# Where VectorE splits the next group's operands inside an up projection group: after two of its eight result additions instead of after four

## What is computed

```python
s = jnp.einsum("thpd,hpnd->thpn", q, keys)          # scores; top 16 of 256 pairs per head give idx and gate
pre = jnp.einsum("td,thkd->thk", xt, down[idx])
act = (jax.nn.gelu(pre.astype(jnp.float32), approximate=False) * gate).astype(xt.dtype)
return jnp.einsum("thk,thkd->td", act, up[idx])     # added to x
```

## Time and profile before

| what | value |
|---|---|
| median of 3 runs | 2968.42 us (2968.40 to 2971.78) |
| the profiled execution | 2967.73 us, of which the span is 2965.8 us |
| PE busy | 2742.1 us, 92% of the span |
| DVE busy | 1888.9 us, 64% |
| ACT busy | 1127.9 us, 38% |
| POOL busy | 1075.9 us, 36% |
| pure groups, layer 0 | 1226.44 to 1477.91 us |
| pure groups, layer 1 | 2693.76 to 2944.84 us |

### The profile page before, as it was taken

The page is one execution under the profiler, slowest core; times in us unless marked ns, Lnnn a source line. Parts: engine busy times, 40 slices in busy tenths (PEclk is TensorE's granted clock), DMA queues, the critical chain, the costliest instruction groups (busy, mean ns, idle before and its releaser), DMA issues.

```text
span 2965.8 us, 55557 instructions
## 1 busy us (share of the span) xinstructions
PE 2742.1 (92%) x20766; PEld 2529.3 (85%) x20766; DVE 1888.9 (64%) x3331; ACT 1127.9 (38%) x1682; POOL 1075.9 (36%) x444
## 2 busy tenths in 40 slices
PE   7899999989987999999988999999999889999997
PEld 5687777889987999999866877778999779999997
DVE  1663562299798554689817526533995975457887
ACT  1312320344487444333303124104445864443332
POOL 0000110478843656433300001004887245663332
PEclk9999999999999999999999999999999999999998
DMA  5222223255544566455452322233555446664543
GB/s 191 101 80 82 103 75 140 88 174 175 170 146 171 199 207 205 155 194 184 143 184 72 104 72 90 88 128 129 170 170 169 152 174 206 198 199 165 195 172 107
DMA packets 145453, 439.50 MB, mean 148 GB/s; under 512 B 62066, under 2 KB 63602, under 8 KB 126772
## 3 DMA queue, kind: packets, MB, share of 16 engines
q1 hardware_dynamic: 132548, 400.84, 39.7%
q10 hardware_dynamic: 12784, 37.00, 3.3%
HBM read 407.10 MB, written 30.15 MB: 147 GB/s over the span
## 4 chain that ended last, share of the span: by engine, by line
PE 61%; DVE 15%; issue 12%; POOL 8%; ACT 2%; DVEq 1%; DMA 0%; POOLq 0%; ACTq 0%; SPq 0%
PE banks L462 60%; POOL DHL L1903 7%; DVE arena L1356 3%; DVE OHE L1356 2%; DVE OHG L1356 2%; DVE ACTS L1356 1%; DVE AHL L1356 1%; ACT arena L983 1%; DVE UHL L1356 1%; POOL arena L1891 1%; DVE hT L1364 1%; DVE arena L1685 0%; DVE arena L1457 0%; DVEq L1356 0%; ACT L983 0%
## 5 line engine op out<-in xcount | busy, mean ns | idle before, releaser
L462 PE MATMUL banks<-HHL,DHL 128*128 128x264 f32 x6816 | 859.4, 287 | 23.6 <-POOL DHL L1903 12.1
L462 PEld LDWEIGHTS banks<-HHL,DHL 128*128 128x128 f32 x6816 | 844.2, 190 | 32.3 <-POOL DHL L1903 16.5
L462 PE MATMUL banks<-AHL,UHL 128*128 128x264 f32 x6144 | 773.3, 286 | 31.6 <-DVE AHL L1356 29.1
L462 PEld LDWEIGHTS banks<-AHL,UHL 128*128 128x128 f32 x6144 | 758.6, 189 | 41.9 <-issue 41.8
L1903 POOL TENSOR_TENSOR DHL<-ring,DHL 128x1024 fp32r<-128x1024 f32 x256 | 657.3, 2572 | 277.8 <-ACT DHL L983 276.0
L1356 DVE TENSOR_TENSOR xT<-xT,banks 128x264 f32<-128x264 f32 x1040 | 402.7, 423 | 388.8 <-PE banks L462 387.9
L462 PE MATMUL banks<-hT,ring 128*128 128x272 f32 (+1 forms) x2048 | 501.8, 403 | 9.7 <-issue 7.9
L1909 POOL TENSOR_TENSOR UHL<-ring,UHL 128x1024 fp32r<-128x1024 f32 x128 | 308.7, 2412 | 538.2 <-ACT UHL L983 538.2
L462 PEld LDWEIGHTS banks<-hT,ring 128*128 128x128 f32 x2048 | 394.4, 196 | 101.7 <-issue 23.1
L983 ACT ACTIVATE UHL<-ring 128x2048 fp32r<-128x2048 f32 x128 | 245.5, 1918 | 509.8 <-PE banks L462 486.7
L983 ACT ACTIVATE arena<-banks 128x264 f32<-128x264 f32 (+6 forms) x226 | 98.7, 455 | 635.9 <-PE banks L462 587.2
(11 more groups left out here) (118 smaller groups left out, 1925.1 us busy)
## 6 DMA issues: line engine op xcount, KB each, us to landing
ring<-down SPq DMA_DIRECT2D x256, 512.0 KB, 3.7
ring<-up SPq DMA_DIRECT2D x128, 1024.0 KB, 4.9
ring<-wm SPq DMA_DIRECT2D x100, 1024.0 KB, 5.0
hT<-second_gates SPq DMA_DIRECT2D x32, 528.0 KB, 4.9
second_gates<-ring ACTq DMA_DIRECT2D x12, 768.0 KB, 3.3
second_gates<-hT ACTq DMA_DIRECT2D x10, 768.0 KB, 3.3
ACTS<-extra_acts SPq DMA_DIRECT2D x2, 2112.0 KB, 9.8
arena<-hs ACTq DMA_DIRECT2D x2, 1280.0 KB, 6.1
```

The lines of the kernel that those rows point to most:

```text
L462: return pe.matmul(out, lhsT, rhs, start=start, stop=stop)
```

## The change

`group` takes two additions, instead of four, ahead of `low(g + 1)` where g is 24 or more; the other six follow. In groups 0 to 23 nothing changes, and no instruction is added or removed.

```diff
                 def group(g, turn, p=None):
 
-                    gather(g, range(0, 4), turn)
+                    ahead = 4 if g < MIXED else 2
+                    gather(g, range(0, ahead), turn)
                     low(g + 1, turn)
                     if p is not None:
                         second_gated(p, p % 4, turn)
-                    gather(g, range(4, 8), turn)
+                    gather(g, range(ahead, KD), turn)
```

## The result

The changed kernel takes 2976.71 us at the median of 13 runs (2972.85 to 2987.47), against 2968.42 (2962.90 to 2971.98, 13 runs) for the kernel before. The ratio is 1.0035, with a 95% interval of 1.0025 to 1.0045: slower by 10 us, 7 to 13. The profiled execution took 2975.39 us, of which the span is 2973.5.

What follows compares the result with a forecast made beforehand. TensorE was held by a 6.23 us chain through ScalarE, GpSimd and VectorE, 0.51 us every second group. Steady groups 0, entry 7.8 and clock falls 2.8 made 10.6 on 2968.42: 2979.0 us, range 2973 to 2984.5.

Steps and rivals of the forecast that it cites:

- The steady groups cost nothing: Groups 26 to 63: VectorE's subtraction still ends 1.08 us behind GpSimd's, the chain stays 6.23 us, change 0 us.
- The six late additions stay covered: Steady groups: six additions behind the split cause no new wait; cover 0.5 us in gated groups, 1.1 in others.
- The new wait at result 6 of groups 24 and 25: Stage entry: result 6 waits for addition 2, now behind the split; +3.9 us a layer, +7.8 in all.
- The price of the pauses: Groups 24 and 25: two clock falls to 1.2 GHz out of four pauses, 1.4 us each, +2.8; bounds 0 and 6.8.
- Sum and time: Whole kernel: 7.8 + 2.8 = 10.6 us slower, median 2979.0 us, next profile about 2978.3.
- The faster rival: Steady groups: earlier start shortens the chain and the 20 waits a layer go; 2953 to 2959 us, chance 0.05.
- the absorbed entry: Groups 24 and 25: the two pauses are absorbed later, 0 to 5 us at most; 2968.5 to 2973.5, chance 0.09.
- VectorE late in the gated groups: Groups 39 to 46: queued additions make VectorE miss GpSimd's end, up to 8 us on top; 2979 to 2987, chance 0.06.
- groups 26 to 63 in 232.5 us as before: Sign of a right forecast: the steady groups of a layer take 232.5 us, unchanged.

Runs made afterwards that it cites:

- experiment 1: The changed kernel, but groups 24 and 25 keep four additions ahead of the split as before; 2966.40 us, ratio 0.9996 to the kernel before.
- experiment 7: On the version of experiment 2, VectorE's weight subtraction waits for the high weights, as GpSimd's does; 2967.61 us, ratio 1.0002 to the kernel before.
- Experiment 5: On the version of experiment 2, VectorE subtracts both weight tiles in one instruction and GpSimd none; 2925.65 us, ratio 0.9860 to the kernel before.
- experiment 2: The changed kernel, but TensorE runs group 24 with room=6 and group 25 with room=8; 2966.58 us, ratio 1.0000 to the kernel before.
- experiment 3: The kernel before, with two additions ahead of the split in groups 24 and 25 alone; 2980.40 us, ratio 1.0044.
- experiment 8: The kernel before, with two additions ahead of the split in group 24 only; 2972.64 us, ratio 1.0018.
- experiment 4: The kernel before, with room=6 for group 24 and room=8 for group 25 and nothing else; 2967.81 us, ratio 1.0002.

## Why the prediction was right

- *The steady groups cost nothing.* Right: experiment 1 has them changed and takes the time of before. The reason given, that VectorE's subtraction runs behind GpSimd's whenever it is issued, holds for starts 0.10 us (experiment 7) to 1.19 us behind GpSimd's. It holds while GpSimd is first, as it always is in the changed kernel's pure groups; experiment 7 shows the other case too, with nearly the same sum. Experiment 5, with GpSimd out of the chain, is where the waits go. VectorE's median instruction grew to 2.68 us and not to 2.9.
- *The six late additions stay covered.* Right. Behind group 26 the waits of 1.4 us and more in the changed kernel's profile (1.40 us in layer 0, 1.55 and 2.24 in layer 1) stand behind a ScalarE instruction that waited for raw weights, and not behind late additions.
- *The new wait at result 6 of groups 24 and 25.* Right in place, count and cause: experiments 1 and 2 take it away in two ways, and experiment 3 produces it alone. The first pause was forecast at 2.29 us and measured at 2.19. The second was forecast at 2.2 and measured at 1.89 and 1.73: with the clock down behind the first pause, TensorE reached it later. Groups 24 and 25 took 18.55 and 18.11 us where 12.86 was the time before and 12.86 + 3.9 = 16.8 the forecast without a clock fall.
- *The price of the pauses.* The mechanism was right; the number of falls was the mis-sized term. I took two falls of 1.4 us. The profiled execution has one behind each of the four pauses. Up to group 26 a layer's two falls cost 1.8 and 1.4 us above the 3.9, and the second reaches on: groups 26 and 27 took 13.21 and 13.50 us where two groups take 12.45 before. So the falls cost about 2.5 us a layer, some 5 in all (an estimate from these windows), where 2.8 was forecast. In the profiled executions of experiments 3 and 8 all four first pauses were followed by a fall too, and cost 0.7 to 1.0 us each; the second pauses of experiment 3, 1.62 and 1.45 us, were not. How many falls a median execution has, the runs don't show.
- *Sum and time.* 10.6 us forecast. The ratio gives 10.4 (7.4 to 13.4), the difference of the medians 8.3. Part of how near this comes is luck. With 5 for the falls the same sum would be some 12.8. The profiled execution lost 14.4 us in groups 24 to 62, and came out 2.9 us under the forecast for the profile because what lies ahead of the change ran 6.1 us faster in it.
- *The faster rival* fell with experiments 1, 2 and 7; *the absorbed entry* with experiment 3; *VectorE late in the gated groups* with experiment 1.

The sign "groups 26 to 63 in 232.5 us as before" did not come true in the profiled execution: 233.29 and 234.74 us up to group 62. The second fall is 0.8 to 1.0 us of it. In layer 1 a pause of 2.24 us before group 45, behind a raw weight transfer that landed late, is 1.1 more; the kernel before has 1.15 us there. The kept traces speak against the change as its cause: before group 45 of the two layers, experiments 1, 2 and 7, with two additions ahead in the steady groups, have 1.26 and 1.40, 1.35 and 1.19, 1.16 and 2.32 us, and experiments 3, 4 and 8, with four, have 1.37 and 1.17, 2.37 and 2.40, 2.27 and 2.71. So this pause varies with either order. Why a transfer lands late stays open.

## What to carry to other kernels

Before an instruction is moved earlier on one engine, look at whether its end moves: an end that stays at a fixed distance behind another engine's end (1.08 us here, for starts from 0.10 to 1.19 us behind the other's) says that an earlier start of that engine buys nothing, short of being first. Look for every wait that counts the moved instructions, above all at the edges of a stage, where a loop's first groups run under an older and tighter count: 2 groups of 64 made the whole loss. An order that is worth nothing under one bound can be worth 55 us once that bound is gone, so take the chain away first and order the rest after.

## What the runs showed of the hardware

When VectorE took over GpSimd's half of the split, the pair was done sooner. Its instruction of 2048 elements lasts 2.29 us, where the two engines together, one behind the other, needed 2.40 + 1.08 us for the same elements. VectorE was 98% busy then (226.42 of 230.40 us), and TensorE's records still cover 230.14 us of the stage; only where VectorE is busy for all of the time, in the gated groups, did most groups take 6.16 us instead of 5.88.

The granted clock fell to 1.2 GHz behind pauses of 1.73 to 2.21 us, all eight of that length at the entry in the profiles of the changed kernel and of experiments 3 and 8, in a stage in which TensorE was otherwise busy nearly all the time. It did not fall behind pauses of 1.45 and 1.62 us. The length of a pause does not decide it alone: of six pauses of 2.24 to 2.71 us before group 45 (changed kernel, experiments 4, 7 and 8), five came with a fall, and the changed kernel's of 2.24 us did not.
